# 13 of 48 modulation slabs per layer moved from the merge levels and the end of the recurrence to the norms at both ends of the feed-forward part

## What is computed

```python
def adaln(cond, w, b):
    return jax.nn.silu(cond) @ w + b
# second block, layer i
mod_lat = adaln(c, mod_w[i], mod_b[i])      # 6 x 1024 values
mod_ctx = adaln(c_ctx, mod_w[i], mod_b[i])
sh1, sc1, g1, sh2, sc2, g2 = jnp.split(mod_lat, 6, axis=-1)
a_lat = modulate(rmsnorm_2(h_lat, norm1_g[i]), sh1, sc1)
```

## Time and profile before

| | |
|---|---|
| runs of the kernel before | 4290.19, 4292.03, 4292.94 us; median 4292.03 |
| profiled execution | 4313.0 us, span 4311.2 us |
| mean granted TensorE clock | 0.921 of 2.4 GHz |
| TensorE matmul / weight load busy | 3846.0 us (89%) / 3323.6 us (77%) |
| VectorE, ScalarE, GpSimd busy | 2454.2, 1702.6, 277.4 us |
| weight loads of line 1382 | 1536, 233 ns each on average |

### The profile page before, as it was taken

One profiled execution on the slowest core, in us unless ns is written; L12 is line 12 of the kernel. 1 busy time (PEld: TensorE's weight loads), 2 busy tenths in 40 slices (PEclk: granted clock), 3 DMA queues, 4 the chain that ended last, 5 costly groups with the idle time before them and its releaser, 6 DMA issues.

```text
span 4311.2 us, 63435 instructions
## 1 busy us (share of the span) xinstructions
PE 3846.0 (89%) x23962; PEld 3323.6 (77%) x23962; DVE 2454.2 (57%) x3551; ACT 1702.6 (39%) x2386; POOL 277.4 (6%) x115
## 2 busy tenths in 40 slices
PE   7899889898979988989695689988989999999998
PEld 6799789898979888989573289984668887676654
DVE  4765544555576534555528365541355555588887
ACT  3431334343451133433224133331334444477776
POOL 0420311000150032000000000000000000000000
PEclk9978789999988779999898899999999999999999
DMA  5431345454532233545220145541135555599996
GB/s 176 136 113 35 121 125 165 137 180 142 170 118 79 64 122 129 176 151 183 84 78 1 39 152 170 177 144 49 44 112 185 175 183 174 175 327 326 336 336 253
DMA packets 180274, 651.53 MB, mean 151 GB/s; under 512 B 20032, under 2 KB 22080, under 8 KB 179472
## 3 DMA queue, kind: packets, MB, share of 16 engines
q1 hardware_dynamic: 179136, 644.24, 45.5%
q0 software_dynamic: 976, 5.05, 0.4%
HBM read 648.16 MB, written 1.05 MB: 151 GB/s over the span
## 4 chain that ended last, share of the span: by engine, by line
PE 81%; DVE 14%; ACT 3%; issue 1%; DMA 1%; ACTq 0%; DVEq 0%; POOL 0%; SPq 0%
PE bank L583 12%; PE bank L584 12%; PE bank L585 12%; PE bank L889 5%; PE bank L1382 5%; PE bank L891 5%; PE bank L890 5%; PE bank L336 4%; PE bank L913 2%; PE bank L915 2%; PE bank L914 2%; DVE arena L1989 2%; PE bank L387 2%; PE bank L438 1%; DVE moe_w_low L1012 1%
## 5 line engine op out<-in xcount | busy, mean ns | idle before, releaser
L1012 DVE TENSOR_TENSOR moe_w_low<-ring,moe_w_high 128x1024 fp32r<-128x1024 f32 x528 | 639.7, 1224 | 261.5 <-ACT moe_w_high L952 253.6
L952 ACT ACTIVATE moe_w_high<-ring 128x1024 fp32r<-128x1024 f32 x528 | 556.0, 1060 | 327.8 <-PE bank L891 215.0
L583 PE MATMUL bank<-ffn_x_high,ffn_w_high 128*128 128x256 f32 x1408 | 402.8, 286 | 58.0 <-DVE ffn_w_low L618 57.6
L618 DVE TENSOR_TENSOR ffn_w_low<-ring,ffn_w_high 128x1024 fp32r<-128x1024 f32 x264 | 321.7, 1222 | 213.8 <-ACT ffn_w_high L603 213.8
L889 PE MATMUL bank<-moe_w_high,picked_high 128*128 128x512 f32 (+4 forms) x968 | 390.3, 403 | 26.9 <-DVE moe_w_low L1012 26.9
L584 PE MATMUL bank<-ffn_x_high,ffn_w_low 128*128 128x256 f32 x1408 | 401.6, 285 | 0.0
L585 PE MATMUL bank<-ffn_x_low,ffn_w_high 128*128 128x256 f32 x1408 | 401.4, 285 | 0.0
L603 ACT ACTIVATE ffn_w_high<-ring 128x1024 fp32r<-128x1024 f32 x264 | 277.5, 1055 | 270.4 <-PE bank L585 270.3
L891 PE MATMUL bank<-moe_w_high,picked_low 128*128 128x512 f32 (+4 forms) x968 | 383.3, 396 | 0.0
L890 PE MATMUL bank<-moe_w_low,picked_high 128*128 128x512 f32 (+4 forms) x968 | 382.8, 395 | 0.0
L583 PEld LDWEIGHTS bank<-ffn_x_high,ffn_w_high 128*128 128x128 f32 x1408 | 273.7, 194 | 60.5 <-issue 59.3
(11 more groups left out here) (438 smaller groups left out, 8800.5 us busy)
## 6 DMA issues: line engine op xcount, KB each, us to landing
ring<-in_moe SPq DMA_DIRECT2D x528, 512.0 KB, 4.9
ring<-in_w_in SPq DMA_DIRECT2D x186, 512.0 KB, 3.5
ring<-in_w_ffn SPq DMA_DIRECT2D x132, 512.0 KB, 3.6
ring<-in_even_ffn SPq DMA_DIRECT2D x132, 512.0 KB, 3.6
ring<-in_mod_w SPq DMA_DIRECT2D x96, 512.0 KB, 3.5
ring<-in_w_branch SPq DMA_DIRECT2D x48, 512.0 KB, 3.5
ring<-in_w_mem SPq DMA_DIRECT2D x32, 512.0 KB, 3.5
ring<-in_even_in SPq DMA_DIRECT2D x20, 512.0 KB, 3.5
```

Of the source, the lines that this page charges most:

```text
L583: nc.tensor.matmul(out, wh, xh, start=start, stop=False, skip_group_check=True)
L618: subtract(low[:, s % 3, :], ring[:, g % RING, :], high[:, s % 3, :], ALU.subtract)\
L952: nc.scalar.activation(high[:, (s0 + q) % 3, :], ring[:, (g0 + q) % RING, :], ACT.Copy).then_inc(c.sem("high_ready"), 1)
L1012: tt(low[:, (s0 + q) % 3, :], ring[:, (g0 + q) % RING, :], high[:, (s0 + q) % 3, :], ALU.subtract)\
```

## The change

Entry 4 of `MODS_AT` goes from 1 to 0, and `MODS_IN` gives five phases in place of three: 17, 11, 7, 6 and 7 slabs. The first phase is now 1 + 8 + 4 + 4 slabs, so the five ahead of the merge levels and the eight after the index scores are gone from there. Six slabs come after the ones products of the feed-forward norm and ahead of the wait for its split; their loads stand between those of `out` and `ffn`. Seven come after the ones products of the next layer's `mix` norm, and in the last layer after those of `final`, ahead of the product for lambda; their loads stand behind those of `ffn`. VectorE's wait for the last modulation slab now names the last of the fifth phase. The number of slabs, products and loads is the same.

```diff
--- before.py
+++ after.py
@@ -42,7 +42,11 @@
 SA_PARTS = (13, 16, 23)
 
 
-MODS_AT = (1, 0, 2, 1, 1, 1, 0)
+MODS_AT = (1, 0, 2, 1, 0, 1, 0)
+
+
+MODS_IN = (17, 11, 7, 6, 7)
+MODS_TO = tuple(sum(MODS_IN[:n]) for n in range(6))
 ROPE_AT = ((0, 1, 2), (3, 4, 5), (6, 7, 8), (9, 10))
 SLAB = KT * P
 TWO_PI_PARTS = (6.28125, 0.0019350051879882812, 3.019916e-07)
@@ -1265,15 +1269,17 @@
         for l in range(DEPTH):
             stream.add(f"dn{l}", dram["w_in"][l], 33, split=True)
             stream.add(f"sa{l}", dram["w_in"][l], 28, first=33, split=True)
-            stream.add(f"mod{l}0", dram["mod_w"][l], MODS - 18)
+            stream.add(f"mod{l}0", dram["mod_w"][l], MODS_IN[0])
             stream.add(f"mem{l}", dram["w_mem"][l], 16, split=True)
-            stream.add(f"mod{l}1", dram["mod_w"][l], 11, first=MODS - 18)
+            stream.add(f"mod{l}1", dram["mod_w"][l], MODS_IN[1], first=MODS_TO[1])
             stream.add(f"xq{l}", dram["w_in"][l], 8, first=61, split=True)
-            stream.add(f"mod{l}2", dram["mod_w"][l], 7, first=MODS - 7)
+            stream.add(f"mod{l}2", dram["mod_w"][l], MODS_IN[2], first=MODS_TO[2])
             stream.add(f"gates{l}", dram["w_in"][l], 24, first=69, split=True)
             stream.add(f"branch{l}", dram["w_branch"][l], 24, split=True)
             stream.add(f"out{l}", dram["w_out"][l], 8, split=True)
+            stream.add(f"mod{l}3", dram["mod_w"][l], MODS_IN[3], first=MODS_TO[3])
             stream.add(f"ffn{l}", dram["w_ffn"][l], 3 * FT, split=True)
+            stream.add(f"mod{l}4", dram["mod_w"][l], MODS_IN[4], first=MODS_TO[4])
         stream.add("even_in", dram["even_in"], 20, split=True)
         stream.add("even_out", dram["even_out"], 8)
         for s in range(2):
@@ -1373,7 +1379,7 @@
 
             def some_mods(l, count):
                 for i in range(mod_next[l], mod_next[l] + count):
-                    part = (i >= MODS - 18) + (i >= MODS - 7)
+                    part = sum(i >= n for n in MODS_TO[1:5])
                     _, g0, _, _, first = stream.phases[f"mod{l}{part}"]
                     g = g0 + i - first
                     pe.wait_ge(c.sem(f"slab_loaded{g % RING}"), 16 * (g // RING + 1))
@@ -1385,6 +1391,8 @@
                 mod_next[l] += count
             for l in range(DEPTH):
                 norm_tensor(te, k, ("mix", l), sq8, KT, T)
+                if l:
+                    some_mods(l - 1, MODS_IN[4])
                 pe.wait_ge(*c.at("split", ("mix", l)))
                 split_gemm_tensor(te, stream, f"dn{l}", l, first_w, first_x)
                 sa_slabs = lambda *part: split_gemm_tensor(te, stream, f"sa{l}", l, first_w, first_x, part=part)
@@ -1568,8 +1576,6 @@
                         for i in range(2):
                             last = mm(ps[:, i * T:i * T + P * (p + 1)], Bq[r, 24 + 2 * (j // 2) + i, p * P:(p + 1) * P], ixk[r, 0:P * (p + 1)], start=True, stop=True)
                         last.then_inc(*te.filled(("score", l, p, j)))
-                some_mods(l, MODS - 18 - mod_next[l])
-
                 norm_tensor(te, k, ("mem", l), sq8, KT, T)
                 pe.wait_ge(*c.at("split", ("mem", l)))
                 split_gemm_tensor(te, stream, f"mem{l}", l, mem_w, mem_x)
@@ -1603,9 +1609,11 @@
                 pe.wait_ge(*c.at("merged_split", (l, KT - 1)))
                 split_gemm_tensor(te, stream, f"out{l}", l, gates_w, merged_x)
                 norm_tensor(te, k, ("ffn", l), sq8, KT, T)
+                some_mods(l, MODS_IN[3])
                 pe.wait_ge(*c.at("split", ("ffn", l)))
                 ffn_tensor(te, stream, f"ffn{l}", l, ffn_w, ffn_x[0], hidden, FT)
             norm_tensor(te, k, "final", sq8, KT, T)
+            some_mods(DEPTH - 1, MODS_IN[4])
 
             te.in_turn = BANKS
             pe.wait_ge(*c.at("lam_prod", "all"))
@@ -2239,7 +2247,7 @@
             dve.wait_ge(*ve.last())
             tt(lamb[:, 0:1], v["lam"][:, 0:1], v["lam"][:, 1:2], ALU.mult).then_inc(*ve.count())
             tt(lamb[:, 1:2], v["lam"][:, 2:3], v["lam"][:, 3:4], ALU.mult).then_inc(*ve.count("lam_prod", "all"))
-            g = stream.phases[f"mod{DEPTH - 1}2"][1] + 6
+            g = stream.phases[f"mod{DEPTH - 1}4"][1] + MODS_IN[4] - 1
             dve.wait_ge(c.sem(f"slab_done{g % RING}"), g // RING + 1)
             tt(mods[:, :, :, :].rearrange("p l n s -> p (l n) s"),
                c.banks[BANKS - 1][:, 0:2 * DEPTH * MODS].rearrange("p (n s) -> p n s", s=2),
```

## The result

| | kernel before | changed kernel |
|---|---|---|
| runs beside each other | 4290.19, 4292.03, 4292.94, 4295.67; median 4292.48 us | 4332.45, 4333.94, 4334.80, 4338.64; median 4334.37 us |
| profiled execution (span) | 4313.0 us (4311.2) | 4334.8 us (4333.0) |
| mean granted clock | 0.921 | 0.918 |

The changed kernel is slower: ratio 1.0098, 95% interval 1.0081 to 1.0116, so 35 to 50 us, and 41.9 us between the medians. The forecast was 4315 us and +23. The two profiled executions differ by 21.8 us. So the first question is why runs and traces disagree by 20 us, and only then which term of the sum was off.

The account below looks back on a forecast made before the run. TensorE's weight-stream matmuls led the chain, but slabs count only where no other engine is as late. 30.6 us added at norms less 7.3 taken away makes 23.3 slower: 4315 us in the runs, range 4301 to 4328.

Parts of the forecast that it names:

- the last of the sum: Whole kernel: profiled 4313.0 us plus 23.3 gives 4336.3; less the 21 us by which profile exceeds runs, 4315 us.
- The added terms: Slabs put at four norms: 6.0 and 3.0 us at feed-forward, 8.5 at layer 1's mixing, 13.1 at final; sum 30.6.
- x: Time the clock stays at 2.4 GHz after a norm's ones matmuls; taken as 2.0, 5.3, 5.2 and 5.3 us.
- the bounds: Total slowdown if the clock fell equally late at every norm: 20.3 us at 5.3 us, 32.4 at 2.0.
- The last norm's 3.6 us of square: Final norm: ScalarE's square of norm e1 queues behind its wait for lambda's matmul, so the 13.1 us late counts in full.
- Taken away: Places that lose slabs: 0.9 us after the recurrence, 6.4 ahead of level 1, nothing at levels 2 to 5; sum 7.3.
- The block behind the recurrence: Eight slabs a layer before the memory norm: ScalarE's square ends the wait anyway, so 0.9 of 45.9 us is gained.
- the slab ahead of level 1: One slab a layer before merge level 1: nothing replaces the wait, so 6.4 us is gained over two layers.
- the eight of levels 2 to 5: Slabs ahead of merge levels 2 to 5, 1.68 us each: VectorE's mask ends the wait, so nothing is gained.
- The rule that spoke for the change: TensorE's clock at the norms: sustained activity releases the throttle, so slabs filling gaps keep it up; about -3 us.
- Rival 1: At the norms, slabs keep the clock at 2.4 GHz; sum -3.1 us, so 4289 us, not slower; 5%.

Follow-up runs that it names:

- square_first: Changed kernel with ScalarE's square of norm e1 issued ahead of the exponential for lambda; median 4328.63 us, ratio 1.0068 to the kernel before.
- d_all: Changed kernel with the 13 moved slabs of each layer left out entirely, loads included; median 4286.30 us, ratio 0.9942 to the kernel before.
- no_mods: Kernel before with all 96 modulation slabs left out, loads included; median 4189.41 us beside 4298.37.
- no_sparse_mods: Kernel before with only the 11 slabs a layer beside the sparse attention left out; median 4276.59 us beside 4298.37, ratio 0.9948.

## Why the prediction was wrong

**The step that failed** is the last of the sum: "it stands 21 us over the median of the runs, 4292.03. I expect 4315 us in the runs". I noted the distance, and then laid the trace's sum on the median of three runs as if these were the kernel's level. The 68 runs put the kernel before at 4303 with groups near 4292, 4303 and 4315. The three runs shown were all of the lowest group, the execution I read of the highest. A time of 4336.3 for the changed profiled execution, which the text gives too, missed its 4334.8 by 1.5 us, and the second pair of traces lies 21.7 us apart.

That accounts for some 11 of the 19 us by which the difference missed, 41.9 us for +23.3; the rest is open. In the longer comparison the forecast lies inside the interval of 21 to 38 us, but near its lower end; in the first one (35 to 50) it does not. The lowest groups of the two kernels, near 4292 and 4323, lie 30 us apart, and none of the changed kernel's ten runs is below 4322. So either its runs miss the short forms more often than those of the kernel before, or the change costs some 30 us and the two pairs of traces fell at 22 by chance.

**The added terms** were right in sum, 32.3 us against 30.6, by errors that cancel, and that is luck. x was 5.3 us at the first feed-forward norm where I took 2.0 from its own row, and about 2.1 at the mixing and the final norm where I took 5.3. A kernel's row gives the time at which the clock fell in that execution, not a property of the norm: in the second trace of the kernel before x was 5.4 us at the first feed-forward norm and 2.2 at the second, where the first trace had 2.0 and 5.2. Both values were in the earlier trace rows, and the bounds (20.3 with every x at 5.3, 32.4 at 2.0) were the right use of them. Six slabs measured 15.39 and 15.36 us for the forecast 15.7, seven 21.67 and 21.65 for 22.0 by x = 2.0. The last norm's 3.6 us of square behind ScalarE's wait were in the sum and were confirmed by square_first.

**Taken away.** The block behind the recurrence was covered, the slab ahead of level 1 was not, and the eight of levels 2 to 5 were covered. Over the two stages the changed kernel's three traces average 1075.9 us and the two of before 1084.4 (sums of the table), 8.5 less for a forecast of 7.3. That is luck as well: the single differences run from 1.2 more to 15.9 less, and the 8.5 are made of a recurrence's stage that was 3 to 17 us shorter and an attention of layer 0 that was 7 to 14 longer, neither of which the sum has. The single terms are smaller than what the clock does to the same stage (423.0 and 436.5 us of the same code), so they are confirmed by the waits and, for the block, by the 0.2 and 0.7 us from the last score product on, not by the lengths of the stages.

**What I had no term for** is that the clock's fall and rise in the two stages with slabs among dense matmuls is not fixed by the code. The changed kernel's three traces all had the sparse attention of layer 0 in a long form (107.2, 113.4, 113.4), before's two had 99.7 twice, and layer 1 was 105.7 three times against 107.1 and 98.6. Whether the change makes the long forms more frequent, or five traces happened to fall so, is open; d_all took the short form in the same code. A stage that is 13.5 us shorter was followed by an attention 6.2 us longer, so where the attention begins in the clock's pattern may matter; that is a guess from lengths, it was not tried, and d_all and the first trace, with equal stages, went on with 98.2 and 107.2.

**The rule that spoke for the change.** The clock fell under full load at every block of slabs (2.1 to 5.3 us into it), so slabs kept it up in no gap. Rival 1 is refuted, and for these slabs the measurement decides against the rule. The Trainium skill, "TensorE: Matmul & The Clock Gate", section on the HAM clock gate, also says that the number of slow matmuls at a start changes from run to run, and that the ramp is under 1% of a typical span, not to be fitted. The runs agree with the size, the groups lie 0.3% to either side of the middle one; slow matmuls at a start were not counted here. But a change worth 0.5% cannot be read without counting that.

## What to carry to other kernels

Work that fills time in which an engine waits costs nothing as long as it fits, and its whole excess once it does not: in a 12.65 us gap five slabs were free at three norms and cost 1.5 us at a fourth, where the clock fell sooner, six cost 2.6 us, and seven in 5.91 us cost 15.8, a quarter of it through ScalarE's queue. Look for the place where the filler is paid now before choosing where to move it: here it was beside the sparse attention (1.0 us a slab by the runs, 1.7 to 2.2 by the stage), and moving eight a layer from there, besides five from ahead of the levels, gave 32 us, where the studied change moved those that were mostly free. And when the profiled execution stands apart from the runs, ask for the spread of the runs first: a median of three told the wrong group.

## What the runs showed of the hardware that was not expected

The same code ran in three groups of times, 4292, 4303 and 4315 us, on one chip as well as over three, with other shares on each. Two-column matmuls with a weight load each, 16 to a slab, keep TensorE busy and yet do not hold its granted clock: a slab takes 1.8 us or 3.4 us. Among dense matmuls with such slabs the clock was low for different lengths from execution to execution, so that one stage of 665 matmuls took 98.6, 105.7, 107.2 or 113.4 us at mean clocks of 0.86, 0.81, 0.79 and 0.74. Without its eleven slabs the same stage took 80.7 to 82.7 us in four cases (no_mods and no_sparse_mods, two layers each). The spread is not theirs alone: the part from norm e1 on, without any slab, took from 2199 to 2209 us over the traces.
